# A hybrid decoder layer on one core: last-level products, state updates and decode sums in another order

## What is computed

```python
def step(S, inp):
    r_t, w_t, k_t, v_t, kk_t, a_t = inp
    sa = jnp.einsum('bhvk,bhk->bhv', S, -kk_t)
    S = S * w_t[:, :, None, :] + sa[..., None] * (kk_t * a_t)[:, :, None, :] + v_t[..., None] * k_t[:, :, None, :]
    return S, jnp.einsum('bhvk,bhk->bhv', S, r_t)
...
mixed = jnp.concatenate([att.reshape(B, T, ATT_WIDTH).astype(jnp.float32), y_rw], axis=-1)
return mixed.astype(x.dtype) @ w_out, k, v, wkv_T.astype(x.dtype)
...
x1 = layer_norm(ALPHA * x + h, ln1_g, ln1_b)
f, conv_T = conv_ffn(x1, conv_prev, w_ffn_in, conv_w, conv_b, w_ffn_out)
y = layer_norm(ALPHA * x1 + f, ln2_g, ln2_b)
```

## Time and profile before

| | us |
|---|---|
| median of 3 runs | 872.43 |
| lowest, highest | 868.4, 874.28 |
| the profiled execution | 872.92 |
| its span, first to last instruction | 871.1 |

### The profile page before, as it was taken

How to read it: one execution, slowest core, us unless ns; L and a number is a source line. 1 busy time by engine, 2 the same in 40 slices (tenths; PEclk the granted TensorE clock), 3 DMA queues, 4 the chain that set the end, 5 groups by cost and what they waited for, 6 DMA issues and landing times.

```text
span 871.1 us, 23141 instructions
## 1 busy us (share of the span) xinstructions
PE 815.2 (94%) x10012; PEld 763.6 (88%) x10012; DVE 494.8 (57%) x764; ACT 330.9 (38%) x569; POOL 274.0 (31%) x121
## 2 busy tenths in 40 slices
PE   6999999999887777899998999999999999999994
PEld 6899889898677676688888999999999999999994
DVE  5588766786577666265354777766667661000037
ACT  5644565454313122433265434333333331111124
POOL 0000000000297670325252444444344434344300
PEclk9999999999999999999998999999999999999997
DMA  7232133152243343703111333223322332333202
GB/s 267 84 97 74 49 98 98 49 198 61 88 116 107 107 126 118 237 15 104 58 54 44 98 113 106 80 91 98 97 86 85 98 88 89 92 88 89 85 2 99
DMA packets 32470, 83.47 MB, mean 96 GB/s; under 512 B 5144, under 2 KB 10456, under 8 KB 31728
## 3 DMA queue, kind: packets, MB, share of 16 engines
q1 hardware_dynamic: 32368, 81.98, 30.7%
HBM read 75.87 MB, written 5.91 MB: 94 GB/s over the span
## 4 chain that ended last, share of the span: by engine, by line
PE 86%; DVE 7%; ACT 3%; issue 2%; POOL 1%; DMA 0%; DVEq 0%; ACTq 0%; POOLq 0%
PE banks L1850 83%; PE banks L1904 1%; DVE z L1241 1%; DVE xx L1241 1%; PE banks L2253 1%; DVE ms L1241 1%; DVE rw L1241 1%; DVE z L1244 1%; POOL wr_lo L697 1%; DVE ssa L1505 1%; ACT x_hi L1149 0%; ACT z L1152 0%; ACT z L1212 0%; DMA w_raw<-in_w 0%; ACT nv L982 0%
## 5 line engine op out<-in xcount | busy, mean ns | idle before, releaser
L1850 PE MATMUL banks<-x_hi,w_hi 128*128 128x264 f32 (+1 forms) x784 | 207.7, 298 | 11.4 <-DVE x_lo L1241 8.9
L1850 PE MATMUL banks<-x_hi,w_lo 128*128 128x264 f32 (+1 forms) x784 | 198.3, 286 | 0.0
L1850 PE MATMUL banks<-x_lo,w_hi 128*128 128x264 f32 (+1 forms) x784 | 198.3, 286 | 0.0
L1850 PEld LDWEIGHTS banks<-x_hi,w_hi 128*128 128x128 f32 x784 | 138.9, 191 | 24.5 <-issue 11.3
L1850 PEld LDWEIGHTS banks<-x_lo,w_hi 128*128 128x128 f32 x784 | 139.1, 192 | 0.1
L1850 PEld LDWEIGHTS banks<-x_hi,w_lo 128*128 128x128 f32 x784 | 138.9, 191 | 0.0
L697 POOL TENSOR_TENSOR w_lo<-w_raw,w_hi 128x1024 fp32r<-128x1024 f32 (+1 forms) x38 | 90.6, 2385 | 152.2 <-ACT w_hi L825 152.0
L697 POOL TENSOR_TENSOR wx_lo<-w_raw,wx_hi 128x1024 fp32r<-128x1024 f32 (+1 forms) x34 | 81.8, 2406 | 100.5 <-ACT wx_hi L825 100.1
L1244 DVE SCALAR_TENSOR_TENSOR z<-z,banks 128x260 f32<-128x260 f32 (+1 forms) x24 | 12.4, 515 | 122.1 <-PE banks L1850 121.9
L1850 PE MATMUL banks<-x_hi,wx_lo 128*128 128x260 f32 x352 | 73.5, 283 | 0.0
L1850 PE MATMUL banks<-x_hi,wx_hi 128*128 128x260 f32 x352 | 73.5, 282 | 0.0
(11 more groups left out here) (254 smaller groups left out, 1713.0 us busy)
## 6 DMA issues: line engine op xcount, KB each, us to landing
w_raw<-in_w SPq DMA_DIRECT2D x87, 512.0 KB, 3.6
w_raw<-in_w SPq DMA_DIRECT2D x16, 448.0 KB, 3.3
kv<-in_ck SPq DMA_DIRECT2D x16, 192.0 KB, 4.1
kv<-in_cv SPq DMA_DIRECT2D x16, 192.0 KB, 3.4
att<-in_x SPq DMA_DIRECT2D x8, 264.0 KB, 6.0
att_out<-att SPq DMA_DIRECT2D x1, 2112.0 KB, 8.9
z<-in_xc SPq DMA_DIRECT2D x2, 1040.0 KB, 6.7
y_out<-z SPq DMA_DIRECT2D x8, 260.0 KB, 2.2
```

The costliest lines, as they stand in the source:

```text
L1850: return pe.matmul(out, l, r, start=start, stop=stop)
```

## The change

- **PE.** In pairs 1 to 3 `chain_step(2n-2)` and `value_terms(n-1)` stand behind the half products of level 5 instead of ahead of them. At a pair's end the full products of level 5 of both groups come first, and `chain_step(2n-1)` and `state_outputs(n-1)` later, behind `start_inverse` of both groups (pairs 1 and 2) or behind `to_tokens(3, 1)` (pair 3). `to_tokens(n, 0)` stands behind the full products.
- **DVE.** `transitions` stand behind the two updates of level 4 instead of ahead of them. `chain_state(2n-2)` stands behind level 5 and not in it. `state_sum(0)` goes from pair 1, level 3, to the end of pair 1; `state_sum(1)` from pair 3, level 3, to behind the transitions of level 4.
- **ACT.** `ny_copy` writes the output `yy` of a chunk right behind that chunk's `nv`. The sigmoid of pair 3 stands ahead of `ny_copy`.
- **SP.** The two weight transfers wait for POOL's seventh step and stand ahead of the copy of the decode row, which goes behind `values_of(3)`.

No instruction is added or removed.

```diff
@@ -653,17 +653,18 @@
         sp.wait_ge(sw_a, 6)
         for v in range(2):
             sp.dma_start(a["swkv_out"][:, 32 * v:32 * v + 32, :], swk[64 * v:64 * v + 64]).then_inc(state_left, 16)
-        sp.wait_ge(sw_y, 1)
-        for v in range(2):
-            sp.dma_start(yrow[:, :].rearrange("b (h k) -> b h k", k=HD)[:, :, 32 * v:32 * v + 32],
-                         ssa[64 * v:64 * v + 64, 1, :]).then_inc(y_landed, 16)
         sp.wait_ge(state_left, 32)
+        sp.wait_ge(sw_a, 7)
         weights(N_IN)
         weights(N_IN + 1)
         sp.wait_ge(bt_ps, 3 * TB - 2)
         sp.dma_start(z[:, 0:CC, :], a["xc"][:, 0:CC, :]).then_inc(z_landed, 16)
         values_of(2)
         values_of(3)
+        sp.wait_ge(sw_y, 1)
+        for v in range(2):
+            sp.dma_start(yrow[:, :].rearrange("b (h k) -> b h k", k=HD)[:, :, 32 * v:32 * v + 32],
+                         ssa[64 * v:64 * v + 64, 1, :]).then_inc(y_landed, 16)
         sp.wait_ge(bt_ps, 3 * TB - 1)
@@ -977,13 +978,12 @@
             for j, b in enumerate((6, 2)):
+                q = 2 * n + j
                 for c in range(CC):
                     x = slice(c * HD, (c + 1) * HD)
-                    ins = ac.activation(nv[:, j, x], banks[:, b, x], ACT.Copy, scale=dec[:, c, 2 * n + j:2 * n + j + 1])
+                    ins = ac.activation(nv[:, j, x], banks[:, b, x], ACT.Copy, scale=dec[:, c, q:q + 1])
                 ins.then_inc(nv_done, 1)
                 own(nv_done)
-            for j, b in enumerate((6, 2)):
-                q = 2 * n + j
                 ac.activation(yy[:, :, q * CH:(q + 1) * CH],
@@ -1038,10 +1038,10 @@
                     token_copy(n, 0)
+                    ac.activation(rw[:, J_G:J_G + 2, :], rw[:, J_G:J_G + 2, :], ACT.Sigmoid).then_inc(lo_act, 1)
+                    own(lo_act)
                 ny_copy(n - 1)
                 if n == TB - 1:
-                    ac.activation(rw[:, J_G:J_G + 2, :], rw[:, J_G:J_G + 2, :], ACT.Sigmoid).then_inc(lo_act, 1)
-                    own(lo_act)
                     late_high(0)
@@ -1526,30 +1526,29 @@
-                if n >= 1 and l == 4:
-                    transitions(n - 1)
                 if n == 1 and l in (2, 5):
                     s_score(2 + l // 4)
-                if (n, l) == (1, 3):
-                    state_sum(0)
...
-                if (n, l) == (3, 3):
-                    state_sum(1)
-                if l == 5 and n >= 1:
-                    chain_state(2 * n - 2)
                 for g in range(2):
                     update(n, l, g)
                     if l == 5 and n + 1 < TB:
                         inverse_start(n + 1, g)
+                if n >= 1 and l == 4:
+                    transitions(n - 1)
+                if (n, l) == (3, 4):
+                    state_sum(1)
...
             if n >= 1:
+                chain_state(2 * n - 2)
+                if n == 1:
+                    state_sum(0)
                 chain_state(2 * n - 1)
                 add_y(n - 1)
@@ -2298,7 +2297,7 @@
-                if n >= 1 and l == 4:
+                if n >= 1 and l == 5:
                     if n >= 2:
                         chain_step(2 * n - 2)
                     value_terms(n - 1)
@@ -2311,25 +2310,24 @@
             if n < TB - 1:
                 inverse_scores(n + 1, 0)
-                to_tokens(n, 0)
                 full_products(n, NLEV - 1, 0)
                 inverse_scores(n + 1, 1)
+                full_products(n, NLEV - 1, 1)
+                to_tokens(n, 0)
+                start_inverse(n + 1, 0)
+                to_tokens(n, 1)
+                start_inverse(n + 1, 1)
                 if n >= 1:
                     chain_step(2 * n - 1)
-                full_products(n, NLEV - 1, 1)
-                start_inverse(n + 1, 0)
-                to_tokens(n, 1)
-                if n >= 1:
                     state_outputs(n - 1)
-                start_inverse(n + 1, 1)
                 to_tokens(n, 2)
...
             else:
+                full_products(n, NLEV - 1, 0)
+                full_products(n, NLEV - 1, 1)
                 to_tokens(n, 1)
-                full_products(n, NLEV - 1, 0)
                 chain_step(2 * n - 1)
-                full_products(n, NLEV - 1, 1)
                 state_outputs(n - 1)
                 to_tokens(n, 2)
```

## The result

| | before | after |
|---|---|---|
| median of 22 runs each, same chip, us | 873.61 | 873.80 |
| lowest, highest | 868.4, 875.24 | 870.77, 878.06 |
| profiled execution, its span | 872.92, 871.1 | 875.52, 873.7 |

The ratio after to before is 1.0027, 95% interval 1.0015 to 1.0040: 2.4 us slower, where the forecast had 3.6 us faster. By both the change is slower by some 0.3%: within the 1% that was called likeliest, but on the other side, and the median lies just above the forecast's range (873.5).

A forecast was written before the change was run, and what follows sets the result against it. PE, holding 86% of the chain, was taken as the bound. Pair 1 -1.5, pair 2 +0.1, pair 3 -3.6 and issue +1.35 gave -3.6 us: 872.92 to 869.3 profiled, median 868.8, range 864.5 to 873.5.

The forecast's parts named there:

- the 1% that was called likeliest: Whole kernel: a result within about 1%, 8.7 us, of no change was given a chance of 0.93.
- In pair 3 the second decode values (1.06, as those in rows 7) also go into the wait: Pair 3, level 4: value terms end 1.4 us later, but 1.06 + 0.7 us of PE work is already done.
- that sum (+ 5.6): End of pair 3: last transposes start 5.6 us after the value terms end, at 352.8 against 356.40, gaining 3.6 us.
- Issue time: PE's waits for instructions, three pairs: of 2.71 us dropped in pair 3, half returns, +1.35, bounds 0 and 2.71.
- the first rival: Dense parts of PE: instruction supply sets the pace, 872.4 to 875 us; sign, issue above 9 us; chance 0.2.
- Decode sum of pair 1, -2.3: Pair 1, level 3: without the reduction the update starts 2.30 us sooner; at the pair's end it costs 0.
- Weights sooner: 0: SP's weight transfers: requesting them earlier gains 0, since the rounding at 352.00 had not waited for its data.
- the rule of turns: DMA engines alternate between queues packet by packet, so removing the weights' megabyte would change little and all 2.71 us return.
- the transposes no longer wait for `yy`: Ends of pairs 1 and 2: full products placed in between remove the waits, -0.3 and -0.7 us.
- the decode row: Rival at the output products: the row lands late and holds POOL's weights up, 1 to 3 us, 875; chance 0.05.
- The wait for `ktok`: End of pair 3: PE would idle some 2 us ahead of the last transposes, ACT being late.
- should only shift: Rest of the kernel after the pairs: paced by PE's products and their sums, it would move without other change.

The follow-up runs named there:

- e8: The changed kernel with the cached values loaded 64 instead of 512 columns wide; 871.79 us, ratio to before 0.9991.
- e11: The changed kernel with the cached values and first half of the attention input held until pair 3's value terms are past; 879.72 us, ratio to before 1.0084.
- e13: e12 with the level part added: transitions behind level 4's updates, chain step and value terms behind level 5's half products; 876.08 us, ratio to before 1.0040.
- e15: The changed kernel with only pair 3's second decode values put back behind the value terms; 872.08 us, ratio to before 0.9980.
- e16: e13 with only pair 3's second decode values put back behind the value terms; 873.83 us, ratio to before 1.0010.
- e5: The kernel before with SP's new order alone (weights sooner, decode row behind the cached values); 872.32 us, ratio to before 0.9995.
- e1: The kernel before with only the two decode sums moved; 876.93 us, ratio to before 1.0054.
- e4: The changed kernel with SP's old order (copy of the decode row ahead of the weights); 879.65 us, ratio to before 1.0077.
- e12: The kernel before with the two decode sums moved, SP's new order and the early sigmoid, all else as before; 869.58 us, ratio to before 0.9962.
- e3: The kernel before with only the pair ends' new order, yy right behind nv, and the early sigmoid; 874.95 us, ratio to before 1.0035.
- e2: The kernel before with only transitions behind level 4's updates, chain step and value terms behind level 5's half products; 876.27 us, ratio to before 1.0053.
- e14: The changed kernel measured once more, unaltered, beside the kernel before; 875.18 us, ratio to before 1.0029.
- e10: The kernel before with the cached values loaded 64 instead of 512 columns wide; 872.18 us, ratio to before 1.0006.
- e7: The changed kernel with 64 small products added at the start, so every later PE record is 128 higher; 879.50 us, ratio to before 1.0075.

## Why the prediction was wrong

- **The step that failed: "In pair 3 the second decode values (1.06, as those in rows 7) also go into the wait"**, which I counted as 1.06 us of PE's work hidden at no cost. I named `values_of(v)` as waiting for `decode_values(v-2)` and did not follow it: the transfers that they release went from 347.8 to 343.2 us, into the moment when PE asks for its next block. The 2.71 us of issue, which the sum let go and gave back by half, became 3.99, with another 0.95 one block earlier. By the sum the value terms of pair 3 end at 343.0 - 1.14 + 5.3 = 347.2; they ended at 352.37, and of these 5.2 us the two stops are 4.9. The rest of that sum (+ 5.6) held, so the last transposes, forecast at 352.8, came at 358.03. Shown by e8, e11, e13, e15 and e16, each of which moves or shrinks these transfers, or lets them go early.
- **"Issue time" was mis-sized.** Taken +1.35 on top of 7.3 - 2.71, so about 5.9 us in all; measured 11.7. The sign of the trouble that I had set (above 9 us, the first rival) holds: instructions set the pace, at 0.2 too small a chance. Its two places, level 4 of pair 1 and the value terms of pair 3, were right too. I had bounded the returning time by the 2.71 of one stop, where the waits removed elsewhere could bring stops where there were none: 1.44 us in pair 1.
- **Decode sum of pair 1, -2.3:** the wait did go from 2.7 to 0.4 us, and the stop at record 6082 took 1.44 of it back. Moved to the pair's end it cost nothing that the trace shows; that part of the step held.
- **"Weights sooner: 0"** was right for the kernel as it was (e5) and wrong for the changed one. Before, SP asked for the weights at 341.09, behind the second decode sum (337.21), and they had landed by 346.02, well ahead of the rounding at 352.00. The change makes that sum run later, at 341.77 in e1 and 345.23 in e4; with SP's old order the request goes with it, to 345.65 and 349.12, and PE waits 4.6 and 3.1 us for `ktok`. I costed the sum's new place for DVE and PE, and did not ask what it releases on SP. That taking the weights away would change little for the instructions, as the forecast read from the rule of turns, is not borne out: without them the stop at 10434 fell from 2.71 to 0.55 us (e5).
- **What held:** no `ssa` on the chain in level 3; the transposes no longer wait for `yy`; the sigmoid ran at 340.75; PE waited 1.2 us for `rw` in pair 2; the decode row was in time (no wait of POOL for it on the chain). In pair 3 the wait for `rw` was covered by a stop for a block (0.95 us at 344.06), so the list has it once, not twice. The wait for `ktok` was 0.9 us, not 2.
- **The output stage, which "should only shift",** lost about 1 us of its own: the granted clock fell there, in 419 to 423 us.

The granted clock is a part of every number here. In after it fell from 2.4 to 1.2 GHz right behind the 3.99 us stop, as these two stretches show (clock is third from the end):

```profile
347.00:351.00 4.00, 0.44 (x25) 0.30 (x16) 1.19 (x3) 0.00 (x0) 0.00 (x0) 1.00 0.64 201
351.00:355.00 4.00, 3.57 (x58) 3.14 (x58) 1.23 (x4) 2.45 (x10) 0.00 (x0) 0.57 0.02 4
```

Before had the same fall, behind its stop of 2.71 us:

```profile
351.00:355.00 4.00, 4.00 (x64) 3.55 (x66) 2.13 (x7) 3.68 (x4) 1.78 (x1) 0.57 1.06 306
```

What after has more is a fall in pair 2 (0.95 in 289.2 to 322.3 us, before 1.00) and the one at 419 us. In e12, with a stop of 0.55 us there, it stayed at 1.00 through both stretches. Over the 31 executions of before beside e5 to e8 the time falls by 5.0 us for each 0.01 of mean granted clock (correlation -0.86); over the four other sets of before the slope is 4.4 to 7.9. e12's executions had 0.9878 on average against 0.9841 of before, the changed kernel's 0.9833: of the 2.8 us between the means of e12 and before, some 2 go with the clock by this slope. That long stops bring the lower clock is argued from where the falls stand, not shown by an experiment, and e15 has a fall at 346.7 us, where PE does not stop for a block.

The stop at record 9154 is 2.85 to 3.67 us in after, e3, e8, e11 and e15, and 1.07 or less in before, e12 and eight others (1.88 in e13, 2.15 in e2). Nothing here was made to move it, but the traces show where it comes from. In after SP issues the writes of the decode state (1 MB) at 320.26 us, PE enters the block before at 321.08, and its packet comes at 325.39; in before the order is the other way round, PE at 321.02, the writes at 321.99, and the packet comes at 323.26. These two stretches, after and before, have a DMA share (second from the end) of 0.97 and 0.71:

```profile
321.08:325.39 4.31, 3.65 (x136) 3.24 (x131) 2.81 (x8) 1.19 (x2) 0.56 (x1) 1.00 0.97 231
...
321.02:323.26 2.24, 2.24 (x87) 1.98 (x83) 0.36 (x2) 1.19 (x2) 1.21 (x1) 1.00 0.71 211
```

In e14, the same kernel as after, the packet came 0.28 us after PE's entry, ahead of the writes' bulk, and there is no stop. So it looks like the same collision, with another transfer; e8 left it whole (3.31) because it shrank the cached values and not these writes. No experiment held the writes back, so this is read from the traces and not tested.

## What to carry to other kernels

When a product is moved ahead, follow what its end releases, through the queues to the transfers, and look what is on the DMA then: decode products whose transfers start 4.6 us sooner cost 0.5%, more than the whole change was to bring. A reduction that is moved to a later place takes along what waits for it, here the request for the weights. Where PE idles without a releaser, count its records; if the stops stand multiples of 256 apart, a removed wait ends at the next of them, and the question becomes what else is on the DMA when the block is asked for. Parts of a change can each be slower alone (e1, e2, e3), since one pays for a wait that another covers (e2's for `yy`), and the best set found here (e12) came from adding them one by one, transfers first.

## What was not expected of the hardware

- A kernel whose every instruction is laid out ahead can be paced by their arrival: 7.3 us of 100 in before and 11.1 in the fastest version, in steps of 256 records. The same block cost 0.55 us with the DMA at 7% (e12) and 3.99 to 4.53 us with it full (after, e13, e14).
- Taking 7/8 of the bytes from the cached values (e8, e10) moved the time by 0.4% in one kernel and by nothing in the other, though the DMA share was 1.0 in both when PE asked for its block. In before the weights and `z` filled it, and not the cached values.
- 64 small products at the very start of the program (e7) put all that follows off by 6.5 us, 0.1 us each; in pair 3, 123 products of the same size run in 2.43 us. Why is open.
